# Square sums of the differential heads: two matmuls on a rounded high and low part instead of one in plain fp32

## The chip, the cores and the metric

One Trainium2 chip, one core of it. The metric is the device time of one execution in microseconds (us). The cores' engines are named as in the profile: PE is TensorE (its weight loads are PEld), ACT is ScalarE, DVE is VectorE, POOL is GpSimd, SP is the engine that issues DMAs.

## The reference, cut to what matters

The reference is two layers of a hybrid trunk. Each layer projects its input, runs three token mixers side by side and merges their outputs:

```python
o_na = neighbourhood_attention(...)          # 8 heads x 64
o_f  = fourier_mix(f_u, fnet_w[l])           # 4 groups x 128
o_d  = diff_attention(qd, k_all, v_all, lam, diff_subln_g[l], lam_init)   # 4 heads, values of 128
y = merge_branches(g, (o_na, o_f, o_d), (na_z, f_z, d_z), w_branch[l], w_out[l])

def diff_attention(...):                     # a = softmax map 1 - lam * softmax map 2
    ...
    return rmsnorm(o, subln_g) * (1.0 - lam_init)

def rmsnorm(x, g):
    return x * lax.rsqrt(jnp.mean(x * x, axis=-1, keepdims=True) + EPS) * g
```

The change touches one thing: the mean of squares over the 128 values of each differential head, for each of 1152 tokens (1024 latent, 128 context). There are 4 heads and 2 layers, so it happens 8 times.

## The kernel before, in words

Activations lie transposed, channels on the 128 partitions and 1152 tokens along the row; a chunk is 384 tokens (`CH`), and there are three (`NC`). Almost all products are made to fp32 accuracy out of the rounded format fp32r: an operand is split into a high part (a copy rounded to fp32r) and a low part (value minus high), and a product takes three matmuls, high by high, low by high and high by low. ACT makes high parts (the copy), DVE or POOL the low ones (a subtraction).

A *unit* (`unit`, L720) is one 128x384 output of the input projection: 8 steps over k with three matmuls each, 24 matmuls. A *job* (`job`, L700) is a whole 128x1152 output, 9 matmuls for each step over k. `unit(c, n, k0, k1)` does only the steps from k0 to k1, and a job can call other work between its steps (`between`, L717).

The phase of the differential heads runs over heads h = 0 to 3 (loop at L1007). PE's order is written out by hand. At the start of a head it turns values into rows (`values_to_rows`), does the gate's three units (z, 0), (z, 1), (z, 2), the first scores (`scores(0)`, L1013) and one more unit; then come nine steps that mix score matmuls, transposes of probabilities (`probs_t`), units of other projections and value products. The square sums of the head before (`square_sums`, L995) stand between unit (z, 0) and unit (z, 1). For the last head of a layer they stand in the first job of the branch projections (loop at L1089), after its step k = 1. They use PSUM banks 3 to 5, which `scores(0)` writes too, so `scores(0)` waits until ACT has read the sums (`sso_read`).

What stands around the sums on the other engines:
- DVE copies the head's output out of PSUM into `obuf` (`out_pair`, L1854).
- ACT squares it (`head_squares`, L1399) into `sqo`. This is behind one piece of high values (`value_high`) and ahead of the evacuation of unit (z, 0). At the layer's end it is ahead of `out_high(2)` and `out_high(3)` (L1486), whose low parts (`out_low`, L1781, on DVE) are the rows that steps k = 2 and k = 3 of the first branch job wait for.
- ACT makes the factor in `head_norm` (L1403): three Ln, one for each chunk, then an Exp over all of them. Each of the two functions loads its own activation table. Then comes the evacuation of unit (z, 1).
- DVE multiplies `obuf` by the factor (`normed_head`, L1786), after the two maxima of the new head's first scores, and later by the gate (`gated_head`, L1792).
- POOL makes low parts of weights (`split_to`, L1949), of queries and keys (L1974 to L1980) and of the cached values (`cached_low`, L1982). Its order is by hand too.
- SP loads the branch inputs. At a layer's end it waits for all square sums (`sso_done`, L654) before it issues the next load of a stored head (`out_load`, L602) and the next weights.

`sqo` shares its place with `e2`, and the factor `rso` shares its place with `xr`.

Of the kernel before, what the change touches and what calls it, by code (L numbers as in the profile page):

```python
# [8 lines left out]
F32 = mybir.dt.float32  # L9
F32R = mybir.dt.float32r  # L10
ALU = mybir.AluOpType
ACT = mybir.ActivationFunctionType
AX = mybir.AxisListType

P = 128
# [196 lines left out]
def build(nc, x_in, cache_na_k, cache_na_v, cache_diff_k, cache_diff_v, cvec, norm_g, w_mod,  # L212
# [90 lines left out]
    pl = Place(na_at)  # L303
    zs2 = pl("zs2", [P, T])
    e1 = pl("e1", [P, 2, T])
    e2 = pl("e2", [P, T])
    aTh = pl("aTh", [P, LT + 1, 2 * P], F32R)
    aTl = pl("aTl", [P, LT + 1, 2 * P], F32R)
# [5 lines left out]
    xc = pl("xc", [P, TL])  # L314
    assert pl.at <= nc.sbuf_usable_end, pl.at - nc.sbuf_usable_end
    rso, sqo = xr, e2
    na_gates, df_zs = (gst, gst2), (zs, zs2)


# [81 lines left out]
    def by_chunk(ap):  # L401
# [5 lines left out]
        un_done u_evac z_tanh z_evac  # L407
        na_s na_b na_e na_p na_pt na_pth na_ptc na_pv na_o df_s df_m df_e df_p df_pt df_pth df_ptc df_pv df_o
        f_store0 f_store1 u_pair pair_copied folded x_done q_done q_copied f_hi f_lo f_ctx
        sqo_ready sso_done sso_read rso_ready out_ready o_load0 o_load1 o_hi o_lo g_load0 g_load1 g_load2 y_added  # L410
        x_load0 x_load1 x_load2 x_load3 y_hi y_lo out_done out_evac y_ready y_store""".split()
    S = namedtuple("Semaphores", names)(*[nc.alloc_semaphore(n) for n in names])
    w_load, o_load, x_load = (S.w_load0, S.w_load1), (S.o_load0, S.o_load1), (S.x_load0, S.x_load1, S.x_load2, S.x_load3)
# [65 lines left out]
    with nc.Block() as block:  # L479
# [217 lines left out]
        def _(pe):  # L697
# [22 lines left out]
            def unit(c, n, k0=0, k1=KT):  # L720

                s, bank = SPLIT_NO[c], BANK[c, n]
                if k0 == 0:
                    if n == 0:
                        pe.wait_ge(S.w_lo, s + 1)
                    if BEFORE[c, n]:
                        pe.wait_ge(*unit_evac(*BEFORE[c, n]))
                for k in range(k0, k1):
                    for a, b in ((whi, hhi), (whi, hlo), (wlo, hhi)):
                        x = mm(ps[:, bank, 0:CH], a[:, s % 2, k, :], b[:, k, n * CH:(n + 1) * CH],  # L730
                               start=(k == 0 and a is whi and b is hhi), stop=(k == KT - 1 and a is wlo))
                if k1 == KT:
                    x.then_inc(unit_done(c, n)[0], 1)
# [111 lines left out]
            for l in range(DEPTH):  # L845
# [149 lines left out]
                def square_sums(u):  # L995

                    pe.wait_ge(S.sqo_ready, u + 1)
                    for c in range(NC):
                        mm(ps[:, 3 + c, 0:CH], ones[:], sqo[:, c * CH:(c + 1) * CH], start=True, stop=True
                           ).then_inc(S.sso_done, 1)  # L1000

                for r in "qkv":
                    if r in "qk":
# [3 lines left out]
                for h in range(HEADS):  # L1007
                    n, u = 2 * HEADS * l + HEADS + h, l * HEADS + h
                    n9, g0, o0 = u * TILES, u * (3 * LT + 1), u * 5
                    z, v = ("z", l, "df", h), ("v", l, "df", h)  # L1010
                    steps = df_steps(l, h)

                    def scores(t):  # L1013

                        if t:
                            pe.wait_ge(S.df_e, 2 * (n9 + t))
                        if t == LT:
                            x = score([(m, ps[:, 3 * m, 0:P]) for m in range(2)], t, TL + PAST, TK)
                        else:
                            for b, (k0, k1) in enumerate(((0, 512), (512, 1024), (1024, 1152))):  # L1020
                                x = score([(m, ps[:, 3 * m + b, 0:k1 - k0]) for m in range(2)], t, k0, k1)
                        x.then_inc(S.df_s, 2)

                    def probs_t(t, g):

                        if g == 0:
                            pe.wait_ge(S.df_p, n9 + t + 1)
                        else:
                            pe.wait_ge(S.df_ptc, g0 + 3 * t + g)
                        tiles = range(4 * g, min(4 * g + 4, TILES)) if t < LT else (0,)  # L1030
                        for j, kt in enumerate(tiles):
                            x = nc.tensor.transpose(ps[:, DF_TURN_BANK[h][t], j * P:(j + 1) * P], e1[:, t % 2, kt * P:(kt + 1) * P], ident[:])  # L1032
                        x.then_inc(S.df_pt, 1)

                    def values(pair):

                        w = 2 * P if pair < 4 else P
                        tiles = [*range(LT), TILES] if pair < 4 else [LT]
                        for j, vtile in enumerate(tiles):
                            for a, b in ((vhi, aTh), (vlo, aTh), (vhi, aTl)):  # L1040
                                x = mm(ps[:, DF_OUT_BANK[h][min(2 * pair + 1, LT)], 0:w], a[:, vtile, :], b[:, j, 0:w],  # L1041
                                       start=(j == 0 and a is vhi and b is aTh),
                                       stop=(j == len(tiles) - 1 and b is aTl))
                        x.then_inc(S.df_pv, 1)

                    values_to_rows(n, v, 0, 1)
                    unit(z, 0)
                    values_to_rows(n, v, 1, 2)
                    values_to_rows(n, v, 2, 0)
                    if h:  # L1050
                        square_sums(u - 1)
                        pe.wait_ge(S.df_o, o0)
                    unit(z, 1)
                    pe.wait_ge(S.x_split, 2 * n + 2)
                    pe.wait_ge(S.v_lo, 3 * n + 3)
                    if h:
                        pe.wait_ge(S.sso_read, NC * u)
                    scores(0)
                    unit(z, 2)
                    unit(*steps[0][0])  # L1060
                    pe.wait_ge(*unit_evac(z, 2))
                    pe.wait_ge(S.vc_lo, n + 1)
                    for t, units in enumerate(steps[1:]):
                        if t:

                            pe.wait_ge(*unit_evac(*steps[t][-1 if DF_TURN_BANK[h][t] == DF_TURN_BANK[h][t - 1] else 0]))
                        probs_t(t, 0)
                        if t < LT:
                            scores(t + 1)
                        if t and t % 2 == 0:  # L1070
                            pe.wait_ge(S.df_o, o0 + t // 2)
                        if t < LT:
                            unit(*units[0], 0, 2)
                            probs_t(t, 1)
                            unit(*units[0], 2, 5)
                            probs_t(t, 2)
                            unit(*units[0], 5, KT)
                        else:
                            unit(*units[0])
                        pe.wait_ge(S.df_ptc, g0 + (3 * (t + 1) if t < LT else 3 * LT + 1))  # L1080
                        if len(units) > 1:
                            unit(*units[1])
                        if t % 2 or t == LT:
                            if len(units) > 1:
                                pe.wait_ge(*unit_evac(*units[0]))
                            values(t // 2)


                for i in range(3 * KT):  # L1089
                    b = i // KT  # L1090
                    tail = {}
                    if i == 0:
                        tail = {1: (lambda: square_sums((l + 1) * HEADS - 1),)}
                    if i == 1:
                        pe.wait_ge(S.sso_read, NC * (l + 1) * HEADS)
                    job(("b", l, "", i), omh[b], oml[b], (S.o_lo, 3 * BK * l + b * BK) if i % KT == 0 else None, tail)
# [16 lines left out]
        def _(act):  # L1113
# [142 lines left out]
            for l in range(DEPTH):  # L1256
# [141 lines left out]

                def head_squares(u):  # L1399
                    act.wait_ge(S.df_o, 5 * (u + 1))  # L1400
                    fn(sqo[:], obuf[:], ACT.Square).then_inc(S.sqo_ready, 1)

                def head_norm(u):  # L1403

# [540 lines left out]
        def _(pool):  # L1945
# [26 lines left out]
            for l in range(DEPTH):  # L1972
# [5 lines left out]
                def key_low(n):  # L1978
                    pool.wait_ge(S.x_hi, 2 * n + 2)
                    g_.tensor_tensor(kl[:], kraw[:], kh[:].bitcast(F32), ALU.subtract).then_inc(S.x_split, 1)  # L1980

                def cached_low(n):  # L1982
                    pool.wait_ge(S.vc_hi, n + 1)
                    g_.tensor_tensor(vlo[:, TILES, :], vraw[:], vhi[:, TILES, :].bitcast(F32), ALU.subtract
                                     ).then_inc(S.vc_lo, 1)
# [27 lines left out]
                key_low(n0)  # L2013
                for h in range(HEADS):
                    n, cs = n0 + h, fillers(l, "df", h)
                    split_to(SPLIT_NO[cs[0]] + 1)
                    cached_low(n)
                    split_to(SPLIT_NO[cs[-1]] + 2)
                    if h + 1 < HEADS:
                        query_low(n + 1)  # L2020
                        key_low(n + 1)
                    split_to(SPLIT_NO[cs[-1]] + 3)
                for i in range(3 * KT):
                    split_to(SPLIT_NO["b", l, "", i] + 2)
                for n in range(NC):
# [113 lines left out]
```

## Time and profile before

| | |
|---|---|
| median of 3 runs | 2939.92 us (2939.52 to 2941.76) |
| span of the profiled execution | 2938.6 us, 44082 instructions |
| DVE busy | 1330.6 us (45%) |
| ACT busy | 1076.5 us (37%) |
| POOL busy | 614.0 us (21%) |
| square sums, all 48 matmul records | 16.8 us busy on PE |

The page gives no other time of the profiled execution than its span. The span lies 1.3 us below the median of the runs. Busy time of PE is the time in which some matmul is under way: matmuls overlap, and the duration of one is its latency, not the pace of a stream. A plain fp32 matmul is recorded twice, so 24 of them give the 48 records.

### The profile page before, as it was taken

The page shows a single profiled execution, that of the slowest core. Times are in us where ns is not written, and L with a number is a line of the kernel's source. Part 1 is how long each engine was busy: PE and PEld are TensorE (multiplying, and loading weights), DVE is VectorE, ACT ScalarE, POOL GpSimd, SP SyncE. Part 2 cuts the span into 40 slices and gives each one's busy share as a digit, 9 for nine tenths or more (in the row PEclk, how much of TensorE's full clock was granted, in tenths as well). Part 3 has the DMA queues.
Part 4 walks back from the last instruction along what each step waited for, and adds up shares of the span by engine and source line. Part 5 has one row for each costly group of instructions (what it writes and reads, how often), then busy time and mean ns, then how long its engine had stood idle before and what let it go on. Part 6 is the DMA issues. An engine that isn't in the chain of part 4 may idle for free.

```text
span 2938.6 us, 44082 instructions
## 1 busy us (share of the span) xinstructions
PE 2877.4 (98%) x18396; PEld 2756.4 (94%) x18396; DVE 1330.6 (45%) x2291; ACT 1076.5 (37%) x1947; POOL 614.0 (21%) x312
## 2 busy tenths in 40 slices
PE   6999999999999999999999999999999999999998
PEld 5999999999999999999999999999999989899997
DVE  4343443123557575446344434421146567554543
ACT  4333333221444544422343333323133444443231
POOL 0221221122221212122431221211221121211242
PEclk9999999999999999999999999999999999999999
DMA  5332224102111102254421121220211111215532
GB/s 224 102 110 82 102 90 137 67 15 78 42 47 47 48 32 94 80 203 141 133 79 65 66 82 39 94 83 22 70 41 45 44 48 47 78 51 183 165 110 94
DMA packets 84278, 248.55 MB, mean 85 GB/s; under 512 B 9201, under 2 KB 30193, under 8 KB 83057
## 3 DMA queue, kind: packets, MB, share of 16 engines
q1 hardware_dynamic: 84080, 245.74, 24.5%
q8 instruction: 146, 2.39, 0.3%
q14 instruction: 52, 0.42, 0.0%
HBM read 191.71 MB, written 54.00 MB: 84 GB/s over the span
## 4 chain that ended last, share of the span: by engine, by line
PE 89%; DVE 5%; ACT 2%; DMA 2%; issue 1%; SPq 1%; DVEq 0%; POOL 0%; POOLq 0%; ACTq 0%
PE ps L730 44%; PE ps L713 18%; PE ps L823 6%; PE ps L769 6%; PE ps L900 3%; PE ps L1041 3%; PE ps L1032 2%; PE ps L961 2%; PE ps L888 2%; PE ps L943 1%; DVE e L1839 1%; DVE stat L1822 1%; ACT e L1435 1%; DMA wmod<-w_mod 1%; DVE aTl L1846 1%
## 5 line engine op out<-in xcount | busy, mean ns | idle before, releaser
L730 PE MATMUL ps<-hhi,whi 128*128 128x384 f32 x2640 | 916.3, 347 | 5.7 <-DVE obuf L1854 3.3
L730 PE MATMUL ps<-hhi,wlo 128*128 128x384 f32 x2640 | 886.3, 336 | 0.0
L730 PE MATMUL ps<-hlo,whi 128*128 128x384 f32 x2640 | 884.1, 335 | 0.0
L1956 POOL TENSOR_TENSOR wlo<-wraw,whi 128x1024 fp32r<-128x1024 f32 (+1 forms) x188 | 415.8, 2212 | 2063.6 <-ACT whi L1127 2063.5
L730 PEld LDWEIGHTS ps<-hhi,whi 128*128 128x128 f32 x2640 | 500.0, 189 | 24.1 <-issue 7.3
L730 PEld LDWEIGHTS ps<-hlo,whi 128*128 128x128 f32 x2640 | 497.1, 188 | 0.9
L730 PEld LDWEIGHTS ps<-hhi,wlo 128*128 128x128 f32 x2640 | 495.9, 188 | 0.0
L1127 ACT ACTIVATE whi<-wraw 128x1024 fp32r<-128x1024 f32 (+1 forms) x188 | 174.5, 928 | 229.9 <-PE ps L713 209.3
L1444 ACT ACTIVATE aTh<-ps 128x512 fp32r<-128x512 f32 (+1 forms) x200 | 96.5, 482 | 278.4 <-PE ps L1032 278.4
L1691 DVE TENSOR_TENSOR ptl<-ps,pth 128x512 fp32r<-128x512 f32 (+1 forms) x144 | 82.1, 611 | 246.8 <-ACT pth L1301 246.6
L1822 DVE TENSOR_REDUCE stat<-ps 128x1 f32<-128x1152 f32 x144 | 176.5, 1231 | 16.9 <-PE ps L769 16.0
L1435 ACT ACTIVATE e<-ps,stat 128x1152 f32<-128x1152 f32 x144 | 162.3, 1128 | 55.9 <-DVE stat L1822 55.9
L1152 ACT ACTIVATE gst<-ps 128x384 f32<-128x384 f32 x144 | 70.5, 490 | 265.3 <-PE ps L730 265.3
L1846 DVE TENSOR_TENSOR aTl<-ps,aTh 128x512 fp32r<-128x512 f32 (+1 forms) x200 | 108.3, 541 | 106.8 <-ACT aTh L1444 106.0
L1291 ACT ACTIVATE sn<-sn,stat 128x512 f32<-128x512 f32 (+1 forms) x144 | 95.9, 666 | 112.5 <-DVE stat L1676 106.6
L713 PE MATMUL ps<-omh,whi 128*128 128x384 f32 x576 | 132.6, 338 | 0.7 <-POOL wlo L1956 0.7
L713 PE MATMUL ps<-omh,wlo 128*128 128x384 f32 x576 | 131.6, 336 | 0.0
L713 PE MATMUL ps<-oml,whi 128*128 128x384 f32 x576 | 131.6, 336 | 0.0
L769 PE MATMUL ps<-kh,qh 64*128 64x128 f32 (+3 forms) x656 | 117.1, 353 | 0.0
L1032 PE MATMUL ps<-ident,e 128*128 128x128 f32 x584 | 100.5, 279 | 11.4 <-DVE aTl L1846 8.8
L769 PE MATMUL ps<-kl,qh 64*128 64x128 f32 (+3 forms) x656 | 109.4, 329 | 0.0
L769 PE MATMUL ps<-kh,ql 64*128 64x128 f32 (+3 forms) x656 | 109.0, 328 | 0.0
(199 smaller groups left out, 4835.8 us busy)
## 6 DMA issues: line engine op xcount, KB each, us to landing
wraw<-w_in SPq DMA_DIRECT2D x128, 512.0 KB, 4.2
gates_dram<-gst SPq DMA_DIRECT2D x48, 576.0 KB, 3.0
gth<-gates_dram SPq DMA_DIRECT2D x48, 576.0 KB, 4.9
mraw<-w_mod SPq DMA_DIRECT2D x32, 512.0 KB, 3.8
wraw<-w_branch SPq DMA_DIRECT2D x48, 256.0 KB, 2.8
bias<-rpb SPq DMA_DIRECT2D x8, 1280.0 KB, 6.0
outs_dram<-obuf SPq DMA_DIRECT2D x16, 576.0 KB, 3.9
oraw<-outs_dram SPq DMA_DIRECT2D x16, 576.0 KB, 3.8
```

The costliest lines, as they stand in the source:

```text
L713: x = mm(ps[:, at + n, 0:CH], a[:, s % 2, k, :], b[k][:, n * CH:(n + 1) * CH], start=(k == 0 and a is whi and b is mhi), stop=(k == kt - 1 ...
L730: x = mm(ps[:, bank, 0:CH], a[:, s % 2, k, :], b[:, k, n * CH:(n + 1) * CH], start=(k == 0 and a is whi and b is hhi), stop=(k == KT - 1 a ...
L769: x = mm(out, a[r, t * P:(t + 1) * P], b[r, k0:k1], start=(i == 0), stop=(i == 2))
L823: x = mm(ps[:, bank, 0:CH], a[:, k, :], b[:, k, n * CH:(n + 1) * CH], start=(k == 0 and a is hi and b is hhi), stop=(k == KT - 1 and a is lo))
L1032: x = nc.tensor.transpose(ps[:, DF_TURN_BANK[h][t], j * P:(j + 1) * P], e1[:, t % 2, kt * P:(kt + 1) * P], ident[:])
L1127: fn(halves(s)[0][:, 0:kt, :], wraw[:, n % 2, 0:kt, :], ACT.Copy).then_inc(S.w_hi, 1)
L1291: fn(sn[:, e, 0:nk], sn[:, e, 0:nk], ACT.Exp, bias=stat[:, e, 1:2], accum_out=stat[:, e, 3:4]).then_inc(S.na_e, 1)
L1435: fn(out, flat[:, 1536 * m:1536 * m + nk], ACT.Exp, bias=stat[:, t % 2, m:m + 1], accum_out=stat[:, t % 2, 2 + m:3 + m]).then_inc(S.df_e, 1)
L1444: fn(aTh[:, 4 * g:4 * g + w, (t % 2) * P:(t % 2 + 1) * P], ps[:, DF_TURN_BANK[h][t], 0:w * P].rearrange("p (t n) -> p t n", n=P), ACT.Copy ...
L1822: v.tensor_reduce(stat[:, t % 2, m:m + 1], flat[:, 1536 * m:1536 * m + nk], AX.X, ALU.max, negate=True).then_inc(S.df_m, 1)
L1846: v.tensor_tensor(aTl[at], ps[:, DF_TURN_BANK[h][t], 0:w * P].rearrange("p (t n) -> p t n", n=P), aTh[at].bitcast(F32), ALU.subtract).then ...
L1956: g_.tensor_tensor(lo[:, 0:kt, :], wraw[:, n % 2, 0:kt, :], hi[:, 0:kt, :].bitcast(F32), ALU.subtract).then_inc(S.w_lo, 1)
```

## The change

The square of a head is split like everything else. After the Square, ACT copies it to `sqh` in the rounded format. POOL makes the low part `sql`, in place of the square. PE then runs, for each chunk, two matmuls of the ones matrix in the rounded format, with the high and the low part, into the same sum. (Ones are exact in that format, so two do in place of three.) In the middle heads, the sums stand after step k = 3 of unit (z, 1) in place of ahead of it; in the first branch job, after step k = 2 in place of k = 1. POOL makes the low part ahead of the cached values of the next head, and for a layer's last head ahead of the branch jobs' low weights. `sqh` lies where `xr` and `rso` lie.

```diff
@@ -303,6 +303,7 @@
     e1 = pl("e1", [P, 2, T])
+    e2_at = pl.at
     e2 = pl("e2", [P, T])
@@ -314,6 +315,8 @@
     rso, sqo = xr, e2
+    sqh = nc.alloc_sbuf_tensor_at("sqh", [P, T], F32R, offset=rope_end)
+    sql = nc.alloc_sbuf_tensor_at("sql", [P, T], F32R, offset=e2_at)
@@ -996,8 +999,10 @@
                     pe.wait_ge(S.sqo_ready, u + 1)
                     for c in range(NC):
-                        mm(ps[:, 3 + c, 0:CH], ones[:], sqo[:, c * CH:(c + 1) * CH], start=True, stop=True
-                           ).then_inc(S.sso_done, 1)
+                        for part in (sqh, sql):
+                            x = mm(ps[:, 3 + c, 0:CH], ones[:].bitcast(F32R), part[:, c * CH:(c + 1) * CH],
+                                   start=(part is sqh), stop=(part is sql))
+                        x.then_inc(S.sso_done, 1)
@@ -1048,9 +1053,11 @@
                     values_to_rows(n, v, 2, 0)
                     if h:
+                        pe.wait_ge(S.df_o, o0)
+                    unit(z, 1, 0, 4)
+                    if h:
                         square_sums(u - 1)
-                        pe.wait_ge(S.df_o, o0)
-                    unit(z, 1)
+                    unit(z, 1, 4, KT)
@@ -1090,7 +1097,7 @@
                     if i == 0:
-                        tail = {1: (lambda: square_sums((l + 1) * HEADS - 1),)}
+                        tail = {2: (lambda: square_sums((l + 1) * HEADS - 1),)}
@@ -1398,7 +1405,9 @@
                 def head_squares(u):
                     act.wait_ge(S.df_o, 5 * (u + 1))
-                    fn(sqo[:], obuf[:], ACT.Square).then_inc(S.sqo_ready, 1)
+                    fn(sqo[:], obuf[:], ACT.Square)
+                    act.drain()
+                    fn(sqh[:], sqo[:], ACT.Copy).then_inc(S.sqh_ready, 1)
@@ -1979,6 +1988,10 @@
+                def squares_low(u):
+                    pool.wait_ge(S.sqh_ready, u + 1)
+                    g_.tensor_tensor(sql[:], sqo[:], sqh[:].bitcast(F32), ALU.subtract).then_inc(S.sqo_ready, 1)
+
@@ -2013,6 +2026,8 @@
                 for h in range(HEADS):
                     n, cs = n0 + h, fillers(l, "df", h)
+                    if h:
+                        squares_low(l * HEADS + h - 1)
                     split_to(SPLIT_NO[cs[0]] + 1)
                     cached_low(n)
@@ -2020,6 +2035,7 @@
                     split_to(SPLIT_NO[cs[-1]] + 3)
+                squares_low((l + 1) * HEADS - 1)
                 for i in range(3 * KT):
                     split_to(SPLIT_NO["b", l, "", i] + 2)
```

## Rows read from the trace of the kernel before

**Rows 1.** The page: span, and PE's busy time, share and instructions.
```profile
span 2938.6 us, 44082 instructions
PE 2877.4 (98%) x18396; PEld 2756.4 (94%) x18396; DVE 1330.6 (45%) x2291; ACT 1076.5 (37%) x1947; POOL 614.0 (21%) x312
```

**Rows 2.** Chain of waits, 862 to 882 us: start, us, engine and line, instructions.
```profile
871.12 1.94 PE ps L999 x6
873.06 4.17 PE ps L730 x24
877.23 1.87 PE ps L769 x14
```

**Rows 3.** Timeline of ACT, same place: start, us, operation, [idle before <-releaser].
```profile
867.54 1.17 ACT L1401 ACTIVATE e<-obuf 128x1152 f32<-128x1152 f32 x1
...
871.84 1.28 ACT L1407 ACT_TABLE_LOAD   x1
873.13 1.53 ACT L1407 ACTIVATE xr<-ps,eps 128x384 f32<-128x384 f32 x3
...
877.27 0.49 ACT L1143 ACTIVATE zs<-ps 128x384 f32<-128x384 f32 x1
```

**Rows 4.** Timeline of ACT at another norm, between the layers.
```profile
1430.09 1.28 ACT L1218 ACT_TABLE_LOAD   x1
1432.23 0.58 ACT L1218 ACTIVATE crstd<-ps,eps 128x384 f32<-128x384 f32 x1 [0.86 <-PE ps L808]
```

**Rows 5.** Timeline of POOL, 855 to 895 us.
```profile
867.05 2.40 POOL L1956 TENSOR_TENSOR wlo<-wraw,whi 128x1024 fp32r<-128x1024 f32 x1 [0.40 <-ACT whi L1127]
...
885.02 3.01 POOL L1956 TENSOR_TENSOR wlo<-wraw,whi 128x1024 fp32r<-128x1024 f32 x1 [15.15 <-ACT whi L1127]
```

**Rows 6.** Line L1976: duration ns min/median/max, first and last start, forms.
```profile
L1976 POOL TENSOR_TENSOR ql<-qraw,qh x16: 2653/2674/3648, 79.4 to 2527.2; 128x1152 fp32r<-128x1152 f32 x16
```

**Rows 7.** Timeline of DVE, 855 to 895 us.
```profile
877.79 0.55 DVE L1652 SCALAR_TENSOR_TENSOR zs<-zs,ps 128x384 f32<-128x384 f32 x1 [5.22 <-ACT zs L1143]
879.15 2.62 DVE L1822 TENSOR_REDUCE stat<-ps 128x1 f32<-128x1152 f32 x2 [0.80 <-PE ps L769]
...
885.69 0.55 DVE L1652 SCALAR_TENSOR_TENSOR zs<-zs,ps 128x384 f32<-128x384 f32 x1
886.33 2.90 DVE L1795 TENSOR_TENSOR obuf<-obuf,zs 128x1152 f32<-128x1152 f32 x1
```

**Rows 8.** Timeline of PE, 879 to 893 us: the head's first probability transposes.
```profile
887.46 0.60 PE L1032 MATMUL ps<-ident,e 128*128 128x128 f32 x4
```

**Rows 9.** Chain of waits at the end of layer 1, 2652 to 2692 us.
```profile
2666.14 3.23 PE ps L713 x18
2669.37 1.94 PE ps L999 x6
2671.31 20.82 PE ps L713 x119
```

**Rows 10.** Timelines of ACT and DVE, same place.
```profile
2666.80 1.16 ACT L1401 ACTIVATE e<-obuf 128x1152 f32<-128x1152 f32 x1
2667.86 2.20 ACT L1397 ACTIVATE omh<-early 128x1152 fp32r<-128x1152 f32 x2
...
2669.05 2.63 DVE L1783 TENSOR_TENSOR oml<-early,omh 128x1152 fp32r<-128x1152 f32 x2 [2.58 <-ACT omh L1397]
```

**Rows 11.** Chain of waits at the end of layer 0, 1225 to 1265 us.
```profile
1244.09 6.32 DMA oraw<-outs_dram
...
1254.18 10.95 PE ps L713 x61
```

**Rows 12.** Busy by stretch: us, PE PEld DVE ACT POOL, granted clock, DMA share, GB/s.
```profile
41.20:44.40 3.20, 3.13 (x10) 3.16 (x11) 3.09 (x5) 1.44 (x2) 0.00 (x0) 0.50 0.18 68
...
2923.50:2925.70 2.20, 0.02 (x1) 0.00 (x0) 1.80 (x4) 0.79 (x2) 0.69 (x1) 0.97 0.00 0
2925.80:2928.00 2.20, 1.65 (x2) 0.50 (x2) 0.00 (x0) 0.97 (x2) 0.41 (x1) 0.50 0.80 304
```

More of the change, by code:

```diff
@@ L409, in build @@
         f_store0 f_store1 u_pair pair_copied folded x_done q_done q_copied f_hi f_lo f_ctx
-        sqo_ready sso_done sso_read rso_ready out_ready o_load0 o_load1 o_hi o_lo g_load0 g_load1 g_load2 y_added
+        sqh_ready sqo_ready sso_done sso_read rso_ready out_ready o_load0 o_load1 o_hi o_lo g_load0 g_load1 g_load2 y_added
         x_load0 x_load1 x_load2 x_load3 y_hi y_lo out_done out_evac y_ready y_store""".split()
```

## The prediction, made before the changed kernel was run

> **What bounds the kernel now.** I read the page first: PE is busy 98% of the span, DVE, ACT and POOL under half [rows 1]. So a microsecond taken from PE's stream counts, and one added to another engine counts only where PE comes to wait for it. Then I read the chain of waits around the sums. In six of the eight places (heads 1 to 3 of both layers; the six are alike to a few hundredths) it is PE alone, without a gap: six matmul records of the sums take 1.94 us, the 24 of a unit 4.17 us, the first scores 1.87 us [rows 2]. The other two places are the ends of the layers, in the first branch job; there too the chain is PE alone [rows 9]. Last, the timelines of the other engines show how far ahead of PE each producer is. PE's span is 2938.6 us, the median of the runs 2939.9; I work out a difference and add it to the median.
>
> **The sums on PE.** Plain fp32: 1.94 us for six records, 0.323 each. After: six matmuls of 384 columns in the rounded format, which is what a unit is made of, 4.17 / 24 = 0.174 each, 1.04 us for six [rows 2]. That is 0.90 less in each of eight places, 7.2 us in all. No row shows the ones matrix as a rounded operand; its bounds are 1.04 (like a unit) and 1.94 (as now). I take 1.04, the nearest shape.
>
> **Middle heads, is the low part there in time?** New on the way to the sums are a copy on ACT and a subtraction on POOL. Square 867.54 to 868.71 [rows 3]; drain and start 0.07 (estimate); copy 1.16, like the Square of the same shape; handoff 0.08 (estimate, from the 0.09 between a copy's end and DVE's start in rows 10); POOL starts at 870.02. It is free then, since its weight split ends at 869.45 [rows 5]. A subtraction of 1152 columns takes 2.67 us in the middle, 3.65 at most [rows 6]. So the low part lands at 872.69, and PE hears of it at 872.77. PE, with the sums moved behind twelve matmuls of the unit, comes to them at 871.12 + 12 x 0.174 = 873.2, where the first may be issued some 0.15 ahead: 873.05. Margin 0.28 us. It holds if the subtraction stays under 2.95; with 3.65 PE waits 0.7. I take no wait. The copy hides in ACT's pause before it can evacuate unit (z, 0), and the cached values that now stand behind the subtraction on POOL are wanted only after two more units; SP's next load of cached values, which waits for them, has a whole head of time.
>
> **Middle heads, what comes later than before.** ACT's three Ln used to run from 873.13 to 874.66. The table load ahead of them does not wait for the sums: in another norm it starts at 1430.09, while the Ln itself idles 0.86 us for PE's sum [rows 4]. So here the load is over by 873.13 as before [rows 3], the first sum is whole at about 873.6 and the Ln end at 875.1. PE asks for that before the first scores, at 873.2 + 1.04 + 12 x 0.174 = 876.3: no wait. The Exp with its load follows, then the evacuation of unit (z, 1), which moves from 877.27 to about 877.7, and DVE's gate product from 877.79 to 878.25 [rows 3, 7]. DVE can begin the maxima at 878.8 in place of 879.15, while PE's scores end 0.90 earlier: DVE gains only 0.35. Its piece for unit (z, 2), the last thing PE waits for before the first transposes, ends at 886.24 - 0.35 = 885.9, and PE comes at 887.46 - 0.90 = 886.56 [rows 7, 8]. So 0.66 us of the slack is left and the 0.90 stays. Six middle heads: -5.4 us, between -5.4 and -1.2 if POOL takes its longest time.
>
> **The ends of the layers.** Here PE comes to step k = 2 directly after 18 matmuls, at 2669.37; before, the sums stood in between until 2671.31 [rows 9]. Step k = 2 needs the low part of row 2, which ACT and DVE make behind the Square: copies from 2667.86, DVE from 2669.05 [rows 10]. With the new copy ahead of them they move by 1.16 + 0.07, so DVE would start at 2670.3. But POOL's subtraction starts at 2669.27 and runs until 2671.94, and the two get in each other's way: DVE's product of 886.33 takes 2.90 us [rows 7] beside a POOL split that runs from 885.02 to 888.03 [rows 5]. The same subtraction as here, two in 2.63 us, takes 1.3 when POOL is idle [rows 10]. Taken as 1.36 alone, the product lost 1.54 of 1.70 us of overlap. DVE is thus nearly still until 2671.94 and hands row 2 over at about 2673.1, row 3 at 2674.4. PE: idle from 2669.4 to 2673.2, step 2 until 2674.75, sums until 2675.8, step 3 until 2677.35. Before, the last step ended at 2671.31 + 18 x 0.174 = 2674.43. Loss 2.9 us at each end. If DVE and POOL did not collide, row 2 would be there at 2671.65 and the loss would be 1.4; if the rows came at no cost the place would gain 0.9.
>
> The Trainium skill (SBUF — State Buffer, on the GpSimd/Vector port) says that whichever of the two starts first keeps the shared port for its whole instruction, and the other fully blocks. By it DVE would make no progress in the overlap rather than a tenth, row 2 would come at 2673.3 or 2673.4, and the loss would be 3.1.
>
> **The clock.** PE's idle stretch here is 3.8 us. At the end of the program the granted clock is still full over 2.2 us without work and half (1.2 GHz) right after it [rows 12]; in the body it is never so long idle. After the stretch at the start, PE ran ten matmuls in 3.2 us at half clock [rows 12] where full clock takes 1.74, so the price is up to 1.5 us. I take 1.4 at each end; the other bound is 0.
>
> **Layer 0's end besides.** SP's next load waits for the sums, is issued at 1244.09 and lands 6.32 us later; a copy, a weight split and its low part behind it let PE go on at 1254.18 [rows 11], though its 54 matmuls from 1244.0 would end at 1253.4: 0.8 us of wait before. The sums end 4.5 us later than now, so the load is issued at 1248.6. It then has an emptier queue than at 1244.09, when two gate loads were under way; between 3.9 us (estimate: in layer 1 ACT took the same load at once 3.9 us after its issue) and 6.32 it lands at 1252.5 to 1254.9, and PE could go on 3.8 later, 1256.3 to 1258.7, against 1256.3 by its own stream. I take nothing more than the 2.9; the bounds are -0.8 and +1.5.
>
> **Sum.** -5.4 + 2 x 2.9 + 2 x 1.4 = +3.2 us: 2943.1. The change takes 7.2 us off PE and gives 10.4 back at the two places where its new copy and subtraction stand ahead of rows that PE needs.
>
> **Rivals.**
> - The clock holds at both ends: +0.4, 2940.3. For it: one place in the start has 2.2 us without a matmul at full clock. Against: 3.8 us is much longer.
> - POOL and DVE do not collide and the clock holds: -5.4 + 2.8 = -2.6, 2937.3. Against it stands the 2.90 of rows 7.
> - The ends hide everything: -7.2, 2932.7. PE would have to find row 2 ready at 2669.4, before ACT has even begun to copy it.
> - Slower: the low part is late in the six middle heads. Place: PE's wait for `sqo_ready` behind step 3 of unit (z, 1). It decides once the subtraction takes over 2.95 us; at 3.65 PE waits 0.7 in each, +3.2 + 4.2 = +7.4, 2947.3. For it: two of the 16 such subtractions took 3.65 (the maximum of rows 6, DVE beside them). Against: DVE's work at this place reads PSUM and the other 14 are even.
> - The rounded ones matmuls cost what the plain ones do: nothing is won, the ends lose 0.9 more each, 2950.
> - The tables. A switch of functions shows as 1.28 us of load with the Ln 1.29 behind its start [rows 3]. If a switch cost 1.4 us more, DVE's piece for (z, 2) would be some 1.4 us later than PE in each middle head and PE would wait there: about +3.2 + 8.6, 2951.7. That is how the Trainium skill has it (ScalarE: Activation LUTs, What ACT_TABLE_LOAD costs: a drain of about 1380 ns on top of 1283). The trace does not agree with it.
>
> **How the numbers follow.** Chances: forecast 0.45, clock holds 0.20, no collision 0.13, nothing given back 0.05, late low part 0.11, no gain from the format 0.04, tables 0.02. A run of this kernel tells 0.2% (5.9 us) from no change, so faster means below 2934.0, slower above 2945.8. Faster 0.05. Slower: 0.17 from the last three and 0.05 from the forecast itself with layer 0's load late and the clock at its worst, 0.22. Within: 0.73. The range 2936 to 2948 holds the forecast with the bounds of clock and load, both milder rivals and the late low part, and leaves out about 0.12.
>
> **What would show it.** PE's six sum matmuls from first start to the next unit's matmul near 1.04 us. No idle of PE ahead of them in the middle heads, and the head's first transposes 0.9 us earlier against the sums' old start. At both layer ends one idle stretch of PE of 3 to 4 us ahead of step k = 2, released by DVE's subtraction L1783, whose first piece takes 2.5 to 3 us, and a granted clock of half behind it. I am wrong if that idle is under 1.5 us, if PE idles ahead of the sums in the middle heads, or if the clock stays full.

## The result, and the profile after

The changed kernel takes 2945.1 us, median of 12 runs (2940.55 to 2948.97), beside 2940.77 for the kernel before (2937.07 to 2942.23). The ratio is 1.0018, with a 95% interval of 1.001 to 1.0025. It is slower, by less than the 0.2% named ahead as the bound of "no change". The forecast was 2943.1, with a range of 2936 to 2948. One later execution of the changed kernel took 3520.72 us at a granted clock of 0.75 and is left out of the medians below.

The page after, to lay beside [rows 1]:

```profile
span 2946.9 us, 44106 instructions
PE 2877.3 (98%) x18396; PEld 2763.8 (94%) x18396; DVE 1333.6 (45%) x2291; ACT 1084.8 (37%) x1955; POOL 636.3 (22%) x320
```

PE has the same number of records (a plain fp32 matmul is two), and its busy time is the same too, though the span grew by 8.3 us. The page cannot say why; the stages can. The profiled execution is the one of 2948.74 us, the second longest of the twelve, so it shows the change from its dearer side; experiment 8 has another profile of the same kernel. To find what each is worth I took the same DVE instruction in both traces and subtracted its start times, ahead of a stage and behind it. The numbers called "offset" below are worked out in that way.

| stage | forecast | offset, after minus before |
|---|---|---|
| start of the program, before anything that changed | 0 | 0 to 3.54: +3.5 |
| six middle heads | -5.4 | -0.88 each: -5.3 |
| weights in the last head of layer 0 | 0 | 0.73 to 1.24: +0.5 |
| end of layer 0 | +4.3 | 1.24 to 4.90: +3.7 |
| end of layer 1 | +4.3 | 2.57 to 8.28: +5.7 |

The first row belongs to this one execution: from 30 to 50 us the granted clock was 0.63 and 0.52 where the profiled execution of before had 0.89 and 0.76, on the same instructions. What is left, 0.15, lies in the Fourier branch of layer 1. Without the first row the sum is +4.8, close to the ratio (1.0018 of 2940 is 5.3).

**A middle head.** The chain of waits after, which answers to [rows 2]: start, us, engine and line, instructions.

```profile
874.66 2.09 PE ps L733 x12
876.75 1.04 PE ps L1003 x6
877.78 2.09 PE ps L733 x12
879.88 1.87 PE ps L772 x15
```

The six sums take 1.04 where they took 1.94, and it is still PE alone. ACT and POOL at the same place (their timelines; the bracket is the idle time before, and who ended it):

```profile
871.08 1.17 ACT L1408 ACTIVATE e<-obuf 128x1152 f32<-128x1152 f32 x1
872.31 1.17 ACT L1410 ACTIVATE sqh<-e 128x1152 fp32r<-128x1152 f32 x1
...
875.37 1.28 ACT L1416 ACT_TABLE_LOAD   x1
877.13 1.52 ACT L1416 ACTIVATE xr<-ps,eps 128x384 f32<-128x384 f32 x3 [0.47 <-PE ps L1003]
```

```profile
873.56 2.68 POOL L1993 TENSOR_TENSOR sql<-e,sqh 128x1152 fp32r<-128x1152 f32 x1 [0.57 <-ACT sqh L1410]
```

With the 3.54 of this execution's start taken off, POOL begins at 870.02 and ends at 872.70, and PE comes to the sums at 873.21: half a microsecond of margin to the matmuls' place, and no idle time of PE. The table load for the Ln starts 1.4 us ahead of the sums, as [rows 4] had it; the Ln alone waits (0.47).

**The end of layer 1.** The chain of waits after, which answers to [rows 9]:

```profile
2670.61 1.17 ACT sqh L1410
2671.78 1.06 ACT omh L1404
...
2672.86 2.84 DVE oml L1792
...
2675.75 3.25 PE ps L716 x9
2679.00 1.92 PE ps L1003 x6
2680.92 14.24 PE ps L716 x80
```

The chain has left PE. It runs over the new copy, the high and the low part of row 2, and only then PE's step k = 2. Where PE stood, it was idle: its own timeline has 3.80 us ahead of that step. POOL and DVE in their timelines, beside [rows 10]:

```profile
2671.86 2.62 POOL L1993 TENSOR_TENSOR sql<-e,sqh 128x1152 fp32r<-128x1152 f32 x1 [0.99 <-ACT sqh L1410]
```

```profile
2672.86 4.10 DVE L1792 TENSOR_TENSOR oml<-early,omh 128x1152 fp32r<-128x1152 f32 x2 [3.80 <-ACT omh L1404]
```

```profile
2675.75 1.33 PE L716 MATMUL ps<-omh,whi 128*128 128x384 f32 x3 [3.80 <-DVE oml L1792]
```

DVE's two subtractions take 4.10 us in place of 2.63, and all of the excess is in the first: 2.84 in the chain, 1.26 left for the second. POOL's runs until 2674.48, 1.62 us into DVE's first. Behind the wait PE is slow as well: nine matmuls take 3.25 us (1.57 at 0.174 each), and the six sums 1.92, as long as the plain ones did. The granted clock (the eighth figure, after the five engines) in three stretches:

```profile
2675.70:2679.00 3.30, 3.25 (x10) 3.25 (x11) 1.26 (x1) 0.00 (x0) 0.00 (x0) 0.50 0.00 0
2679.00:2681.00 2.00, 2.00 (x7) 2.00 (x7) 0.00 (x0) 1.21 (x3) 0.00 (x0) 0.50 0.00 0
2682.50:2686.00 3.50, 3.50 (x22) 3.50 (x21) 3.07 (x3) 2.60 (x3) 0.00 (x0) 1.00 0.89 318
```

It is the lower level, 1.2 GHz, for at least 5.3 us, and full again behind it. Wider stretches (0.56 over 2674 to 2678, 0.90 over 2681 to 2682.5) put its ends at about 2674.5 and 2681.3: 6.8 us, the first 1.3 of them while PE still waited.

**The end of layer 0**, which answers to [rows 11]:

```profile
1244.17 2.84 DVE oml L1792
...
1247.06 2.72 PE ps L716 x9
1249.78 1.71 PE ps L1003 x6
1251.49 10.68 PE ps L716 x61
```

The shape is the same, with less of the low clock (2.72 and 1.71). The load of the next stored head was issued at 1251.59 and had landed by 1255.31, when ACT, 0.63 us idle, began to copy it. PE's chain does not stop for it; before, it did.

### The profile page after: what moved, and what is told of

It reads as the page before. It is cut to its first block, busy times and chain, and to the rows that moved or that the text cites. A ratio compares the mean times of both kernels' runs of the same rounds, so it can differ in the third digit from the quotient of the medians.

```text
span 2946.9 us, 44106 instructions
## 1 busy us (share of the span) xinstructions
PE 2877.3 (98%) x18396; PEld 2763.8 (94%) x18396; DVE 1333.6 (45%) x2291; ACT 1084.8 (37%) x1955; POOL 636.3 (22%) x320
## 4 chain that ended last, share of the span: by engine, by line
PE 88%; DVE 6%; ACT 2%; DMA 2%; issue 1%; SPq 1%; DVEq 0%; POOL 0%; ACTq 0%; POOLq 0%
PE ps L733 43%; PE ps L716 18%; PE ps L826 6%; PE ps L772 6%; PE ps L903 3%; PE ps L1046 3%; PE ps L1037 2%; PE ps L964 2%; PE ps L891 2%; PE ps L946 1%; DMA wraw<-w_in 1%; DVE e L1848 1%; ACT e L1444 1%; DVE stat L1831 1%; DVE aTl L1855 1%
## 5 line engine op out<-in xcount | busy, mean ns | idle before, releaser
L716 PEld LDWEIGHTS ps<-omh,whi 128*128 128x128 f32 x576 | 103.7, 189 | 8.2 <-DVE oml L1792 8.2
```

The costliest lines, as they stand in the source:

```text
L716: x = mm(ps[:, at + n, 0:CH], a[:, s % 2, k, :], b[k][:, n * CH:(n + 1) * CH], start=(k == 0 and a is whi and b is mhi), stop=(k == kt - 1 ...
```

## The experiments

Their diffs are against the changed kernel; three dots stand for lines left out. Each ratio is to the kernel before, timed beside it. Where losses of a stage are given, they are offsets as above.

**1. Only the middle heads (ends_plain).** The last head of a layer keeps the plain sums at their old place.

```diff
-                        tail = {2: (lambda: square_sums((l + 1) * HEADS - 1),)}
+                        tail = {1: (lambda: plain_sums((l + 1) * HEADS - 1),)}
...
-                head_squares((l + 1) * HEADS - 1)
+                plain_squares((l + 1) * HEADS - 1)
...
-                squares_low((l + 1) * HEADS - 1)
```

> The change in the six middle heads alone; both layer ends keep the plain fp32 sums after step k = 1. Theory (the gain sits in the middle heads, the loss at the ends): each middle head ends 0.9 us earlier against before, one of them gives some 0.5 back in layer 0's last head where weights land late; no idle of PE in the first branch job, full clock there. -4.9 us, ratio 0.998. Rival (the changed run's gain in the middle heads is only the spread between executions, or is eaten downstream): ratio 1.000, no fall of the offset at the heads.

Measured: 2934.84 us, ratio 0.9981 [0.9973, 0.999]. Each middle head stands at -0.88, which makes 5.3 us, and the medians are 5.1 apart: the gain of the format is real and keeps. At the end of layer 1 the chain is again PE alone and the offset stays where it was.

The trace also gains at two places of which no line was edited. At the end of layer 0 it is 1.0: the load behind the sums landed within 4.3 us of its issue, where it took 6.32 in [rows 11], and PE did not wait for the weights. Whether the earlier heads bring that, or before's load was unlucky, is open. Between the layers, at 1526 us, it is 1.5. PE is idle there for 2.44 us in every profile of this document. Its first matmul behind the wait and a stretch, in the kernel before:

```profile
1526.03 0.65 PE L730 MATMUL ps<-hhi,whi 128*128 128x384 f32 x1 [2.44 <-POOL wlo L1956]
```

```profile
1526.00:1529.00 3.00, 2.97 (x9) 2.97 (x10) 0.00 (x0) 2.88 (x3) 2.36 (x2) 0.52 0.51 175
```

And the same stretch in this kernel, where the wait ends at 1524.68:

```profile
1526.00:1529.00 3.00, 3.00 (x20) 3.00 (x19) 0.00 (x0) 1.65 (x2) 3.00 (x2) 1.00 0.42 164
```

Behind the same wait the clock fell to half in nine of the twelve profiled executions, the kernel before among them, and stayed full in three (experiments 1, 4 and 7). The repeat of experiment 4 has it low: this one belongs to the execution and not to the program.

**2. Only the ends (middle_plain).** The middle heads keep the plain sums and their place; the ends are as changed.

```diff
                     if h:
+                        plain_sums(u - 1)
                         pe.wait_ge(S.df_o, o0)
-                    unit(z, 1, 0, 4)
-                    if h:
-                        square_sums(u - 1)
-                    unit(z, 1, 4, KT)
+                    unit(z, 1)
...
```

> The change at the two layer ends alone; middle heads as before. Theory: 3.8 us of PE idle ahead of step k = 2 at each end and half clock behind it, +3.7 and +5.9 us as in the changed kernel, together +9.6, ratio 1.003. Rival (part of that loss hangs on the middle heads having come early, since the loads had less time): under +7, the idle shorter than 3 us.

Measured: 2950.78 us, ratio 1.0039 [1.0023, 1.0054]: +10.8 by the medians (four runs). Experiments 1 and 2 add up to +5.7, and the whole change measured +4.3 by medians and +5.3 by the ratio: to within about 1.5 us nothing shows that the two parts hang on each other. The loss in the trace is 3.7 at layer 0 and 4.6 at layer 1. In the view of the waits (us, times, largest):

```profile
PE ps L716 <- DVE oml L1801: 7.6, 2, 3.8
```

**3. The ends without POOL's subtraction (ends_no_low).**

```diff
+                        for i, part in enumerate((sqh, sqh if u % HEADS == HEADS - 1 else sql)):
...
-                squares_low((l + 1) * HEADS - 1)
```

This kernel leaves out the low part of a layer's last head: PE reads the high part twice, so these sums come out twice as large. PE does the same number of matmuls.

> As the changed kernel, but at the layer ends POOL makes no low part and PE reads the high part twice (the low part is left out of the layer's last head). Theory (DVE and POOL collide): DVE's first subtraction L1792 takes 1.36 us in place of 2.8, PE's idle ahead of step k = 2 falls from 3.8 to about 2.3 us, each end loses 1.4 us with the clock at full and up to 1.5 more if it falls. Rival (the copy alone makes the row late): idle stays 3.8. Second rival (the loss comes through SP's load that waits for the sums): the branch jobs' third weights still hold PE, loss stays near 3.7 in layer 0.

Measured: 2940.06 us, ratio 1.0002 [0.9993, 1.0011]. The end of layer 1 in the chain:

```profile
2665.80 1.17 ACT sqh L1413
2666.97 1.06 ACT omh L1407
...
2668.05 1.37 DVE oml L1795
...
2669.46 2.13 PE ps L716 x9
2671.59 1.92 PE ps L1006 x6
```

With POOL silent DVE's piece takes 1.37 in place of 2.84, and each of the two waits is 1.5 us shorter: 2.3 us. Experiment 6 says what these are made of. The sums still take 1.92: the clock was at the lower level for 3.4 us at each end, behind a wait of 2.3 us. The losses are 2.2 and 3.3.

**4. The wait filled with work (ends_filled).** PE runs 21 matmuls that nobody reads where it would be idle.

```diff
+                def filler():
+                    ...
+                    for j in range(21):
+                        mm(ps[:, 6, 0:CH], whi[:, s % 2, 0, :], omh[0][0][:, 0:CH], start=True, stop=True)
-                        tail = {2: ...
+                        tail = {1: (filler,), 2: ...
```

> As the changed kernel, with 21 matmuls of 384 columns into an unused PSUM bank after step k = 1 of the first branch job, 3.65 us that fill PE's wait for row 2; nothing reads them. Theory (beyond the 2.9 us of late rows the rest is the clock): granted clock 1.00 throughout, step 2 in 1.56 us and sums in 1.04, each end loses 2.9: -0.8 in layer 0 and -3.0 in layer 1 against the changed kernel, -3.8 us in all. Rival (the clock does not decide, PE just has more to do): time the same as the changed kernel or longer.

Measured: 2945.07 us, ratio 1.0017 [1.0008, 1.0026], no better than the changed kernel. At the ends it did what it was meant to; the chain at layer 1's end:

```profile
2671.46 2.91 DVE oml L1800
...
2674.42 1.84 PE ps L716 x9
2676.26 1.04 PE ps L1003 x6
```

Row 2 comes as late as ever, but the matmuls behind it run at full clock, and the losses are 2.2 and 3.2 in place of 3.7 and 5.7. But the clock fell at another place, in the Fourier branch of layer 1. Timeline of PE, and stretches:

```profile
1980.71 1.16 PE L946 MATMUL ps<-tab_c,uT 128*128 128x256 f32 x4 [2.27 <-DVE xdif L1758]
```

```profile
1978.00:1981.00 3.00, 0.72 (x4) 0.41 (x3) 1.10 (x4) 1.60 (x3) 1.33 (x1) 1.00 0.03 11
1981.00:1985.00 4.00, 4.00 (x15) 3.81 (x15) 1.07 (x3) 0.38 (x1) 1.03 (x1) 0.58 0.45 127
```

That costs +2.8 of the 4.0 that the filling saved at the ends. The theory, full clock throughout and 3.8 us less, missed. That the median does not move at all these traces do not explain: the two profiled executions differ in more places, and the changed kernel's was one of its longest.

**5. The sums back at the old place (middle_early).**

```diff
                     if h:
+                        square_sums(u - 1)
                         pe.wait_ge(S.df_o, o0)
-                    unit(z, 1, 0, 4)
-                    if h:
-                        square_sums(u - 1)
-                    unit(z, 1, 4, KT)
+                    unit(z, 1)
```

> As the changed kernel, but the sums of the middle heads stand where they did, ahead of unit (z, 1). Theory (the low part lands some 1.65 us after PE would come): PE idles 1.6 to 1.7 us ahead of the sums in each middle head, released by POOL's L1993 subtraction; against the changed kernel +1.65 each, +9.9 us in all. Rival (POOL is early enough, the move costs or gains nothing): same as the changed kernel.

Measured: 2957.85 us, ratio 1.006 [1.0047, 1.0074]. Waits and chain:

```profile
PE ps L1003 <- POOL sql L1991: 9.5, 6, 1.6
```

```profile
873.52 2.64 POOL sql L1991
...
876.21 1.30 PE ps L1003 x6
```

Six waits of 1.6 us, and the sums behind a wait take 1.30 in place of 1.04. Each head is about 1.8 us worse than with the sums behind step 3. The move of half a unit is what lets the gain through (by itself it is worth nothing, experiment 6): the new low part is on no path only because of it.

**6. The move alone (shift_only).** Plain sums, no copy, no low part, but both new places.

```diff
-                        for part in (sqh, sql):
-                            x = mm(... ones[:].bitcast(F32R), part[...], ...)
+                        mm(ps[:, 3 + c, 0:CH], ones[:], sqo[:, c * CH:(c + 1) * CH], start=True, stop=True
...
-                    act.drain()
-                    fn(sqh[:], sqo[:], ACT.Copy).then_inc(S.sqh_ready, 1)
...
```

> The places of the changed kernel with the sums of the kernel before (plain fp32, no copy, no low part). Theory: middle heads neither gain nor lose more than 0.1 us (the Ln end 2 us later but PE asks for them later still); at the ends PE waits about 1.0 us for row 2, then has full clock: +1.0 each, +2 us against before. Rival (moving the sums is what loses time at the ends, not the copy): the ends lose 3 us or more each.

Measured: 2942.67 us, ratio 1.0007 [0.9997, 1.0016]. The middle heads gain and lose nothing. Each end has one wait of 1.1 us; at layer 1:

```profile
2669.72 1.37 DVE oml L1788
...
2671.14 1.83 PE ps L716 x9
2672.96 1.94 PE ps L1002 x6
```

Even with nothing new on ACT and POOL, step k = 2 waits 1.1 us once the sums no longer stand ahead of it: the plain sums of before had hidden the making of row 2. The clock stays full behind 1.1 us. The losses are 0.4 at layer 0, where the old wait for weights is gone, and 1.3 at layer 1. So the wait of 3.8 is 1.1 (cover gone) plus 1.2 (the copy) plus 1.5 (DVE beside POOL).

**7. The fastest version (ends_plain_weights).** Experiment 1, and SP issues the weights of a layer's last head ahead of the store and the four loads of stored heads.

```diff
+                    if h == HEADS - 1:
+                        weights_to(CHUNK[fillers(l, "df", h)[0]] + 3)
                     if h:
                         sp.wait_ge(S.out_ready, l * HEADS + h)
```

> The change in the middle heads alone, and SP issues the second filler's weights of a layer's last head ahead of the store and the four loads of stored heads. Theory (these weights land 0.5 us later against PE once the heads come early): PE's idle of 0.69 us at the transposes of layer 0's last head goes to zero and with it the 0.17 of before; 0.7 less than with the middle heads alone, -5.6 us against before, ratio 0.998. Rival (the weights land late whatever the order): no difference to the kernel without this edit.

Measured: 2933.47 us, ratio 0.9978 [0.9969, 0.9987]. Over the transposes in the last head of layer 0 this version's offset falls from -1.78 to -2.18, experiment 1's from -0.27 to -0.38: the edit is worth 0.3 us there, in one execution of each. PE's idle ahead of them is gone, but it was only 0.07 in experiment 1, not the 0.69 that the edit was made for. The medians are 1.4 us apart and the intervals of experiments 1 and 7 overlap, so a gain of the weights alone is not shown. Against the kernel before the version is 0.2% faster.

**8 and 9. Changed and filled again, timed side by side (changed_again, filled_again).** No edits.

> The changed kernel unaltered, once more, beside its filled form on the same chip. Theory (the clock falls behind each 3.8 us of idle at the layer ends in every execution): two stretches of half clock at the ends again, 3.4 to 6.8 us of it each; +4 to +6 us against before, ratio 1.0018. Rival (it was that execution's own): full clock at an end.

> The filled form unaltered, once more: 21 unread matmuls in PE's wait at each layer end. Theory (the clock costs 1.4 to 3 us at each end and the filling saves it): median 3 to 4.5 us below the changed kernel's of the same chip, full clock at both ends in the profile. Rival (the clock falls somewhere else then, or the first comparison's equal medians hold): medians within 1.5 us of each other.

Measured: 2944.8 us, 1.0016 [1.0007, 1.0025], and 2943.71 us, 1.0012 [1.0003, 1.0021]. The medians are 1.1 us apart, so it is the rival of the filled form that holds, not the 3 to 4.5 us of the theory. In the changed kernel the clock was low for only 3.4 us at each end; a stretch and the chain at layer 1's end:

```profile
2672.30:2675.50 3.20, 3.20 (x10) 3.20 (x11) 1.14 (x1) 0.00 (x0) 0.00 (x0) 0.50 0.00 1
```

```profile
2672.23 3.25 PE ps L716 x9
2675.48 1.19 PE ps L1003 x6
```

The sums take 1.19 here and 1.92 in the first profile, in the same program: nothing in the code decides how long the clock stays down. The losses are 3.7 and 4.7. In this profile, of an execution of 2943.62 us, PE is not idle at the transposes in the last head of layer 0, and without the program's start (+1.1) the sum of all stages is +2.7. The filled kernel lost 2.2 and 3.3 at the ends and 2.7 once more behind its 2.2 us wait in the Fourier branch. So the clock fell there in both profiles of the filled kernel; in the two of the changed kernel the same wait is at most 1.24 us and the clock stays full. Why the wait is a microsecond longer in the filled kernel was not tried.

**10. The rows first (ends_rows_first).** At a layer's end ACT copies rows 2 and 3 ahead of the Square, and the sums stand after step k = 3.

```diff
-                        tail = {2: ...
+                        tail = {3: ...
-                head_squares((l + 1) * HEADS - 1)
                 out_high(2)
                 out_high(3)
+                head_squares((l + 1) * HEADS - 1)
```

> As the changed kernel, but at the layer ends ACT copies rows 2 and 3 ahead of the Square and its copy, and PE does the sums after step k = 3. Theory (what loses time at the ends is the place of the new work ahead of the rows): no idle ahead of step 2, full clock; the sums wait about 1.6 us for POOL's low part and the next job 1.2 us for the Ln; each end loses about 2 us against before in place of 3.7 and 5.9. Rival (POOL's subtraction and its collision cost the same wherever they stand): the ends lose 3.5 us or more each.

Measured: 2941.62 us, ratio 1.0005 [0.9996, 1.0014]. PE's waits at the two ends:

```profile
PE ps L1003 <- POOL sql L1993: 2.2, 2, 1.1
PE ps L716 <- ACT xr L1416: 1.8, 2, 0.9
PE ps L716 <- DVE oml L1792: 0.4, 2, 0.2
```

The wait of 3.8 is gone and two smaller ones stand in its place, 1.1 for POOL's low part and 0.9 for the Ln, which frees the bank. The losses are 1.4 and 3.7, where the theory had about 2 each with full clock. The larger one has the half clock in it again, behind the pair of waits (1.1 and 0.9 with 1.3 us of sums between them); behind the same pair in layer 0 the clock stayed full:

```profile
2672.40:2674.00 1.60, 1.58 (x5) 1.58 (x6) 0.00 (x0) 1.56 (x2) 0.00 (x0) 0.56 0.85 216
```

The end has no room for the longer chain from Square to sums in either order; the plain sums are the shorter way there.

## Why the prediction came out as it did, step by step

- **Sums at 1.04 us.** Right, to the hundredth; a head gained 0.88 us against the forecast 0.90.
- **The low part in time.** Right. POOL's start was forecast at 870.02 and came there; its end at 872.69 and came at 872.70; PE at 873.2 and came at 873.21 (all with the start's 3.54 taken off). Experiment 5 shows that the wait it avoids is real. The rival with 3.65 us for the subtraction did not come: the eight took 2.62 to 2.68.
- **Ln, evacuation and maxima behind it.** Right. The Ln were to end at 875.1 and end at 875.11; DVE begins the maxima at 878.5 in place of the forecast 878.8, so DVE gained 0.64 and not 0.35. The rival of a table switch that costs 1.4 us more is out: the Exp starts 1.29 behind its load here as before. That is not what the Trainium skill says (ScalarE: Activation LUTs, What ACT_TABLE_LOAD costs).
- **The weights of the last head.** A term of 0 that came out at 0.5, in this one execution. The step saw that DVE gains less than PE and looked only at what PE waits for inside the same head. In the last head of layer 0, SP's weights stand behind the store of the normed head. The gated product that releases the store starts 0.98 us later than in the trace of before, where the offset is 0.73 (0.24 of the gain missing), and the load takes longer:

```profile
1135.08 8.72 DMA wraw<-w_in
```

```profile
1146.14 0.66 PE L1037 MATMUL ps<-ident,e 128*128 128x128 f32 x4 [0.69 <-DVE aTl L1855]
```

  Before it was 8.45 us and PE waited 0.17. So 0.5 us went back here. But in changed_again, the same program, PE does not wait at this place and the offset falls by 0.2, and in experiment 1, with the same middle heads, PE waits 0.07. The 0.5 is not a price that each execution pays.
- **The wait at the ends.** Right: 3.8 us at each, and the sum of its causes too (experiments 3 and 6: 1.5 for the collision, 1.2 for the copy, 1.1 for the cover). In the overlap of 1.62 us DVE lost 2.84 - 1.36 = 1.48, so it made about a tenth of its pace, as the 2.90 of [rows 7] had it. The ends of POOL's instructions are rough in the profile, so none at all is not excluded. By the Trainium skill (SBUF — State Buffer, SBUF: two separate sides) it would have made none; at 0.14 us between the two this changes nothing.
- **The clock: right as a mechanism, too small as a bound.** I took 1.4 us at each end from a stretch of 3.2 us at half clock [rows 12], with 1.5 as the most. The filled kernel has the late rows at full clock and loses 2.2 and 3.2; the changed kernel loses 3.7 and 5.7, and 3.7 and 4.7 in changed_again. So the clock costs 1.5 us three times and 2.5 once. The price goes with how long the clock stays down, 3.4 or 6.8 us in otherwise equal places. The bound of 1.5 was one observation taken for a maximum. The step also says that PE is never so long idle in the body. For the 2.2 us that it compares with, that is misread: the trace of before has a wait of 2.44 us at 1526, with half clock behind it (experiment 1). It would have been the nearer row, and it showed that less than 3.8 us can be enough.
- **The load of layer 0.** It was to come 3.9 to 6.3 us after its issue; it came at most 3.7 after. The wait for weights of 0.8 us in the kernel before was absorbed, the lower bound of the step. I had taken nothing. That wait is missing in experiment 1 as well, whose code at this end is that of before, so the new ends are not the only way to be rid of it.

Term by term against this execution: -5.3 (forecast -5.4), +0.5 (0), +3.7 (4.3), +5.7 (4.3). The balance was right in sign and mechanism, about 1.5 us too kind for this execution and 0.5 too harsh for changed_again's (+2.7). The changed kernel's runs spread more than before (8.4 us against 5.2), and their length follows the granted clock that is listed for each. In its 22 runs without the one of 3520.72, those at 0.996 took 2940.6 to 2940.8 us, at 0.995 2941.9 to 2943.6, at 0.994 2943.9 to 2946.6, at 0.993 2946.2 to 2949.0. In which stage the clock was low these figures do not tell; the profiles have it low in the start, at 1526 and at the ends.

## What to carry to other kernels

Moving sums to a cheaper format pays when the longer chain of splitting fits in a stage with slack, and the consumer is moved to where the new part has landed; at the ends of stages, where the next operand is made just in time, the old slow form was cover, and the same edit loses more than it gains there. So apply such a change place by place, and price each place on its own. And when PE gets a new wait of two microseconds or more, count with the half clock behind it, as a range: it did not come each time, and its length was not always the same.

## What the runs showed of the hardware that was not expected

- The clock fell to 1.2 GHz behind idle stretches of TensorE of 2.2 and 2.3 us (experiments 3, 4 and 9), not only behind the 3.8 us of the changed kernel. Behind the same 2.44 us at 1526 it fell in nine executions and stayed full in three. It stayed full behind single stretches of 1.1 and 1.24 us; behind a pair of 1.1 and 0.9 it fell at one end and not at the other (experiment 10). At [rows 12] it was full over 2.2 us without work and half right behind.
- It came back after 3.4 us at some of these places and 6.8 us at another, in the same program. The first cost 1.5 us, the second 2.5.
- Behind a wait, even a short one at full clock, the first six or nine matmuls take 0.26 us more in the chain (1.30 for 1.04; 1.83 for 1.57). It is paid once: the first matmul takes 0.44 us from start to end (experiment 10), where in a stream each adds 0.174.
- Work that nobody reads kept the clock up where it stood (experiment 4), but the median hardly followed: 2945.07 filled and 2945.1 changed, and 1.1 us apart in the second pair.
